# Top-16 search moved in among the query products, one-hots in four operations, and another order of loads

## The reference

```python
mod = cond @ w_ada[l] + b_ada[l]                 # 6 * 1024 values, sh1, sc1, g1, sh2, sc2, g2
q = (hf @ w_q).reshape(T, PEER_HEADS, 2, D_HALF) # 8 heads, 2 halves of 128
s = jnp.einsum("thpd,hpkd->thpk", q, sub_keys)   # 128 scores per half
top_v, top_i = lax.top_k(s, PEER_TOPK)           # the first top-16, 16 per token
comb = top_v[:, :, 0, :, None] + top_v[:, :, 1, None, :]   # 256 sums a head
best_v, best_j = lax.top_k(comb.reshape(T, PEER_HEADS, 256), PEER_TOPK)   # the second
i1 = jnp.take_along_axis(top_i[:, :, 0], best_j // PEER_TOPK, axis=-1)
i2 = jnp.take_along_axis(top_i[:, :, 1], best_j % PEER_TOPK, axis=-1)
idx, gate = i1 * N_KEYS + i2, jax.nn.softmax(best_v)       # 128 experts a token
a = jnp.einsum("tmd,td->tm", u_tab[idx], x)
y = jnp.einsum("tm,tmd->td", gate * jax.nn.gelu(a, approximate=False), v_tab[idx])
```

## Time and profile before

| what | us |
|---|---|
| runs shown, median (lowest, highest) | 3184.18 (3183.21, 3186.78) |
| profiled execution | 3189.15 |
| its span, granted clock 0.987 | 3187.3 |
| PE busy | 3091.1 |
| DVE busy | 2457.8 |
| POOL busy | 1185.7 |
| ACT busy | 1118.5 |

### The profile page before, as it was taken

One profiled execution on the slowest core, in us unless ns is written; L12 is line 12 of the kernel. 1 busy time (PEld: TensorE's weight loads), 2 busy tenths in 40 slices (PEclk: granted clock), 3 DMA queues, 4 the chain that ended last, 5 costly groups with the idle time before them and its releaser, 6 DMA issues.

```text
span 3187.3 us, 54768 instructions
## 1 busy us (share of the span) xinstructions
PE 3091.1 (97%) x16200; PEld 2682.7 (84%) x16200; DVE 2457.8 (77%) x5952; ACT 1118.5 (35%) x1590; POOL 1185.7 (37%) x765
## 2 busy tenths in 40 slices
PE   6989999999999999999999999999999999999998
PEld 4668888778888899999975788888788889999997
DVE  7981999859995488999977239951799926889987
ACT  3333322234443333333343332223344433333333
POOL 0033445420001366766700334544000024667674
PEclk8999999999999999999999999999999999999999
DMA  6162666445556799999921224444455578999996
GB/s 254 62 216 101 241 231 240 165 139 188 215 207 256 254 362 361 360 361 363 374 91 40 85 82 142 147 145 141 149 218 210 189 287 293 362 358 361 361 371 238
DMA packets 278481, 734.76 MB, mean 231 GB/s; under 512 B 36064, under 2 KB 118368, under 8 KB 276448
## 3 DMA queue, kind: packets, MB, share of 16 engines
q1 hardware_dynamic: 186688, 462.03, 41.7%
q0 software_dynamic: 50688, 151.18, 12.8%
q10 hardware_dynamic: 40992, 120.34, 9.6%
HBM read 613.85 MB, written 119.54 MB: 230 GB/s over the span
## 4 chain that ended last, share of the span: by engine, by line
PE 54%; POOL 18%; issue 14%; DVE 10%; DMA 2%; ACTq 1%; ACT 1%; DVEq 0%; SPq 0%; POOLq 0%
PE bank L507 30%; PE bank L511 15%; POOL z_pad L934 9%; POOL u_pad L928 5%; PE bank L616 3%; POOL z_pad L928 2%; POOL scratch L928 2%; PE bank L528 2%; DVE scratch L1285 2%; PE bank L427 1%; ACTq L826 1%; DVE h L1266 1%; DVE h L1263 1%; PE bank L451 1%; DVE h L1265 1%
## 5 line engine op out<-in xcount | busy, mean ns | idle before, releaser
L507 PE MATMUL bank<-h_hi,w_hi 128*128 128x512 f32 x2528 | 997.9, 395 | 19.2 <-ACT norm_tmp L807 16.3
L673 ACT ACTIVATE w_hi<-ring 128x1024 fp32r<-128x1024 f32 x584 | 615.0, 1053 | 1116.0 <-PE bank L511 1036.8
L507 PE MATMUL bank<-h_lo,w_hi 128*128 128x512 f32 x2528 | 988.2, 391 | 0.0
L913 POOL TENSOR_TENSOR w_lo<-ring,w_hi 128x1024 fp32r<-128x1024 f32 x172 | 442.8, 2575 | 844.2 <-ACT w_hi L673 844.1
L633 PE MATMUL bank<-v_lo,w_hi 128*128 128x368 f32 x2032 | 670.5, 330 | 0.0
L633 PE MATMUL bank<-v_hi,w_hi 128*128 128x368 f32 x2032 | 665.2, 327 | 2.7 <-DVE v_lo L1439 1.8
L511 PE MATMUL bank<-h_hi,w_lo 128*128 128x512 f32 x2528 | 624.3, 389 | 0.0
L507 PEld LDWEIGHTS bank<-h_hi,w_hi 128*128 128x128 f32 x2528 | 476.9, 189 | 119.4 <-ACT w_hi L673 19.1
L507 PEld LDWEIGHTS bank<-h_lo,w_hi 128*128 128x128 f32 x2528 | 476.7, 189 | 97.1
L511 PEld LDWEIGHTS bank<-h_hi,w_lo 128*128 128x128 f32 x2528 | 474.5, 188 | 98.6
L934 POOL DMA_INDIRECT z_pad<-ga_scratch,z_pad x288 | 374.0, 1299 | 155.0 <-issue 86.9
(11 more groups left out here) (184 smaller groups left out, 2885.0 us busy)
## 6 DMA issues: line engine op xcount, KB each, us to landing
ring<-u_t SPq DMA_DIRECT2D x256, 512.0 KB
ring<-v_t SPq DMA_DIRECT2D x256, 512.0 KB
ga_scratch<-norm_tmp ACTq DMA_DIRECT2D x256, 256.0 KB, 2.0
g_scratch<-scratch ACTq DMA_DIRECT2D x12, 4096.0 KB, 13.8
scratch<-ga_scratch SPq DMA_DIRECT2D x256, 192.0 KB
scratch<-ada_t SPq DMA_DIRECT2D x76, 512.0 KB, 5.8
scratch<-g_scratch SPq DMA_DIRECT2D x32, 768.0 KB
keys<-g_scratch SPq DMA_DIRECT2D x32, 768.0 KB
```

The source lines that it names most:

```text
L507: pe.matmul(to, w_hi[:, b, k * P:(k + 1) * P], part_h[:, k, :], start=(k == 0 and part_h is h_hi), stop=False)
L673: return act.activation(to, of, ACT.Copy)
L913: pool.tensor_tensor(w_lo[:, n % 2, :], ring[:, n % RING, :], w_hi[:, n % 2, :].bitcast(F32), ALU.subtract).then_inc(tile_used[n % RING], 1)
```

## The change

Five things change.

1. PE multiplies a segment with its keys right behind the query product two tiles later (`score(n - 2)`), all four token tiles at once, into banks 0 and 1. ACT copies it one step later (`copy_score`). DVE takes the first top-16 of two segments, 8 rows, as soon as both are there.
2. The second top-16 looks at 100 sums a head instead of 256: the first 3 ranks with all 16, the other 13 with the first 4.
3. The look-up of both halves is one comparison and one product over 4096 fp16 elements, then additions of halves.
4. The one-hots of a chunk come from four instructions of 1024 elements. `hot1` now has two tokens side by side, so that PE reads every second fp16.
5. The last eight slices of layer 0 leave the query stage. They take the first turn of the eight slots, and layer 1's 48 follow, four for each four up chunks, starting at the second four. DVE uses them in groups of 5, 5 and 4.

```diff
     NEXT_SLOTS = 8
-    NEXT_FROM = 3
-    NEXT_ROUNDS = (N_ADA - NEXT_SLOTS) // RING
+    NEXT_FROM, PER_ROUND = 1, 4
+    OWN_ADA = KC
+    N_NEXT = OWN_ADA + N_ADA
+    NEXT_ROUNDS = (N_NEXT - NEXT_SLOTS) // PER_ROUND
...
+                def load_own(s):
+
+                    sp.wait_ge(next_used[s], N_NEXT // NEXT_SLOTS * l + 1)
+                    sp.dma_start(ada_next[:, s, :], ada_t[l, N_ADA - OWN_ADA + s]).then_inc(next_landed[s], 16)
...
                 up_rounds(0, 1)
                 with sp.If(l < LAST):
-                    sp.wait_ge(score_ready, 4 * TT * l + 4 * TT)
+                    sp.wait_ge(score_ready, SEGS * l + SEGS)
                     for s in range(NEXT_SLOTS):
-                        load_next(0 * l, s)
+                        load_own(s)
                     settle(sp)
-                    up_rounds(1, NEXT_FROM)
-                    with sp.Fori(0, NEXT_ROUNDS // 2) as q:
-                        for half in range(2):
-                            for s in range(RING):
-                                load_next(q + 1, RING * half + s)
-                            up_round(2 * q + (NEXT_FROM + half))
+                    with sp.Fori(0, NEXT_ROUNDS // 4) as q:
+                        for half in range(4):
+                            for i in range(PER_ROUND * half, PER_ROUND * (half + 1)):
+                                load_next(2 * q + (i // NEXT_SLOTS + 1), i % NEXT_SLOTS)
+                            up_round(4 * q + (NEXT_FROM + half))
...
+                def score(s):
+
+                    pe.wait_ge(q_ready, N_WQ * l + (s + 1))
+                    if s >= 2:
+                        pe.wait_ge(score_ready, SEGS * l + (s - 1))
+                    for a in range(TT):
+                        mm = pe.matmul(bank[:, s % 2, a * P:(a + 1) * P], q_t[:, s, a * P:(a + 1) * P], keys_v[:, s, :],
+                                       start=True, stop=True)
+                    mm.then_inc(score_product, 1)
...
                     product(l, 0, stages["wq"] + n, bank[:, 2 + n % 6, :])
...
+                    score(n - 2)
+                score(N_WQ - 2)
+                score(N_WQ - 1)
...
                 for n in range(N_WQ):
                     hi(0, stages["wq"] + n + 2)
                     copy(q_t[:, n, :], bank[:, 2 + n % 6, :]).then_inc(q_ready, 1)
...
+                    if n >= 3:
+                        copy_score(n - 3)
+                for s in range(N_WQ - 3, N_WQ):
+                    copy_score(s)
...
-                with dve.If(l < 1):
-                    for n in range(KC):
-                        modulate_later(3 * KC + n)
-                wait_later(LATER)
-                add_bias(5 * KC, KC)
...
+                for pair in range(SEGS // 2):
...
+                    dve.wait_ge(score_ready, SEGS * l + (2 * pair + 2))
+                    settle(dve)
+                    top16(PAIR, lambda n: scores[:, seg(n)[1], seg(n)[0], :], lambda n: big_s[:, n, :],
+                          lambda n: vals[:, seg(n)[0], seg(n)[1], :], lambda n: idx_u[:, seg(n)[0], seg(n)[1], :])
...
                     top16(HEADS, lambda s: big_c[:, s, :], lambda s: sc_c[:, s, :], lambda s: best[:, s, :],
                           lambda s: bj_v[:, s, :])
-                    next_modulation(3 if a < TT - 1 else 2)
...
+                    next_modulation(5)
...
+                    link(dve.tensor_tensor(eq_4, ranks.unsqueeze(2).to_broadcast(shape4),
+                                           iota_rank.unsqueeze(1).to_broadcast(shape4), ALU.is_equal))
+                    link(dve.tensor_tensor(eq_4, eq_4, idx_h.unsqueeze(3).to_broadcast(shape4), ALU.mult))
+                    next_modulation(5)
+                    half = TOPK // 2
+                    while half > 1:
+                        link(dve.tensor_tensor(eq_4[:, :, 0:half, :], eq_4[:, :, 0:half, :], eq_4[:, :, half:2 * half, :],
+                                               ALU.add))
+                        half //= 2
...
-                        for j in range(TOK):
-                            t = RING * TOK * r + (s * TOK + j)
-                            col = bass.ds(t, 1)
-                            dve.tensor_scalar(hot2[:, b, j, :], iota_b[:, :], i2_t[:, col], None, ALU.is_equal)
-                            for q, g_part in enumerate((ghi_t, glo_t)):
-                                ins = dve.tensor_scalar(hot1[:, b, j, q, :], iota_b[:, :], i1_t[:, col], g_part[:, col],
-                                                        ALU.is_equal, ALU.mult)
-                        ins.then_inc(hot_ready, 1)
...
+                        dve.tensor_tensor(hot1[:, b, 1, :, :, :], table, along(i1_t), ALU.is_equal).then_inc(hot_step, 1)
+                        dve.tensor_tensor(hot2[:, b, :, :], iota_b[:, :].unsqueeze(1).to_broadcast([P, TOK, P]),
+                                          i2_t[:, cols].unsqueeze(2).to_broadcast([P, TOK, P]), ALU.is_equal)
+                        dve.wait_ge(hot_step, LATE * l + RING * r + s + 1)
+                        dve.tensor_tensor(hot1[:, b, 0, :, :, :], hot1[:, b, 1, :, :, :], along(ghi_t), ALU.mult)
+                        dve.tensor_tensor(hot1[:, b, 1, :, :, :], hot1[:, b, 1, :, :, :], along(glo_t), ALU.mult)\
+                           .then_inc(hot_ready, 1)
```

More of the change, by code:

```diff
@@ L614, in _ @@
                             to = bank[:, 2 + 2 * b + j // PER_BANK, (j % PER_BANK) * P:(j % PER_BANK + 1) * P]
+                            g, i = j // SIDE, j % SIDE
                             for q in range(2):
-                                mm = pe.matmul(to, hot2[:, b, j, :], hot1[:, b, j, q, :], start=(q == 0), stop=(q == 1))
+                                mm = pe.matmul(to, hot2[:, b, j, :], hot1[:, b, q, g, :, i], start=(q == 0), stop=(q == 1))
                         mm.then_inc(gate_product, 1)
@@ L791, in _, with copy_score @@
                 shift_hi(2 * l + 1, 3 * KC)
+                def copy_score(s):
+                    act.wait_ge(score_product, SEGS * l + (s + 1))
+                    copy(scores[:, :, s, :], bank[:, s % 2, :].rearrange("p (a k) -> p a k", k=P)).then_inc(score_ready, 1)
                 for n in range(N_WQ):
@@ L794, in _ @@
                     copy(q_t[:, n, :], bank[:, 2 + n % 6, :]).then_inc(q_ready, 1)
-                for s in range(LATER_SLOTS):
-                    act.wait_ge(later_used[s], LATER // LATER_SLOTS + 1)
-                for a in range(TT):
-                    for b in range(4):
-                        act.wait_ge(score_product, 4 * TT * l + (4 * a + b + 1))
-                        copy(scores[:, a, 4 * b:4 * b + 4, :],
-                             bank[:, 4 * (a % 2) + b, :].rearrange("p (s k) -> p s k", k=P)).then_inc(score_ready, 1)
+                    if n >= 3:
+                        copy_score(n - 3)
+                for s in range(N_WQ - 3, N_WQ):
+                    copy_score(s)
                 def gelu(r, s):
@@ L1287, in next_modulation @@
                                .then_inc(next_used[slot], 1)
                     nexts[0] += n
-                for a in range(TT):
-                    dve.wait_ge(score_ready, 4 * TT * l + 4 * (a + 1))
-                    settle(dve)
-                    sc_a = scores[:, a, :, :]
-                    sc_c = sc_a.rearrange("p s k -> p (s k)").rearrange("p (s k) -> p s k", k=TOPK * TOPK)
-                    top16(SEGS, lambda s: sc_a[:, s, :], lambda s: big_s[:, s, :], lambda s: vals[:, s, :],
-                          lambda s: idx_u[:, s, :])
-                    next_modulation(4 if a < TT - 1 else 3)
-                    link(dve.tensor_tensor(big_4, v2[:, :, 0, :].unsqueeze(3).to_broadcast(shape4),
-                                           v2[:, :, 1, :].unsqueeze(2).to_broadcast(shape4), ALU.add))
+                    if nexts[0] - n < OWN_ADA <= nexts[0]:
+                        settle(dve)
+                        with dve.If(l < LAST):
+                            for slot in range(OWN_ADA):
+                                dve.wait_ge(next_used[slot], N_NEXT // NEXT_SLOTS * l + 2)
+                            settle(dve)
+                        add_bias(5 * KC, KC)
@@ new lines, in _ @@
+                    count(dve.tensor_copy(idx_h[:, :, :], idx_u[:, :, a, :]))
+                    count(dve.tensor_copy(j_f, bj))
+                    dve.wait_ge(dve_step, STEPS * l + (FIRST + steps[0] - 2))
+                    count(dve.tensor_copy(ja_f, ja_u))
+                    link(dve.tensor_copy(jb_f, jb_u))
+                    link(dve.scalar_tensor_tensor(ja_f, jb_f, float(ROWS_WIDE - at // NARROW), ja_f, ALU.add, ALU.max))
+                    count(dve.tensor_copy(ranks_2[:, :, 0, :], heads(ja_f)))
@@ L1318, in _ @@
+                    for e, to in enumerate((i1_f, i2_f)):
+                        ins = dve.tensor_tensor(heads(to[:, a, :]), eq_2[:, :, e, 0, :], eq_2[:, :, e, 1, :], ALU.add)
+                        count(ins)
```

(3 more changed lines are left out.)

138 lines of the change are left out of this document (73 added, 65 removed).

## The result

| | before | after |
|---|---|---|
| median of runs, us (lowest, highest, number) | 3185.48 (3183.21, 3188.43, 4) | 3210.80 (3209.55, 3215.13, 4) |
| profiled execution | 3189.15 | 3211.41 |
| its span, granted clock | 3187.3, 0.987 | 3209.6, 0.984 |
| layer 0's up stage, first up product to first one-hot matmul | 360.08 | 381.43 |
| the same in layer 1 | 355.10 | 355.10 |

What follows compares the result with a forecast made beforehand. PE was taken to bound the kernel, other engines mattering only where PE waits. Terms 22.3 + 2.2 - 5.0 + 0.9 gave +20.4 us, put on the median 3184.18: 3204 us, range 3193 to 3215.

Steps and rivals of the forecast that it cites:

- One-hots: In the 96 one-hot chunks PE sets the pace at 6.45 us, DVE needs at most 6.1: 0 us.
- Rival 3: SP's gate stops PE, but the one-hot chunks give back their 9 us: 3195 us, chance 0.04.
- Moving operand with a step of two: PE reading hot1 at every second fp16 in the small matmuls costs nothing: 0 us.
- The other end, +88: PE reading the spaced one-hot operand at half pace in all 96 chunks would cost 88 us.
- Scores amid the products: At the query stage's end, saved idle time returns as waits on ACT's copies: +0.4 us a layer.
- Both top-16s: In the up stage DVE's lighter top-16 work stays hidden, as ACT still asks at chunk 56: no gain.
- SP's queue: Layer 0's fifth u_t tile waits behind gated slice requests, so PE stops 22.3 us; with clock and old stop, +19.5 us.
- The lower bound of 18 for the stop: Shortest forecast PE stop before layer 0's fifth up chunk: 18 us, with 9.3 us a pair and no queueing.
- Lower clock: After the stop in layer 0's up stage PE runs at its lower level for a while: +2.2 us.
- The stop before 588: PE's old 3.1 us wait in layer 0's up stage goes, with 1.9 more: 5.0 us given back.
- Rival 1: SP's gate does not bite, DVE having used slot 3 by 336.7: 3180 us, chance 0.07, plus 0.03 for faster.
- Rival 2: New one-hots cost PE or DVE: +88 us (3292) for half-pace reads or +370 for slow operations; chance 0.05 together.

Runs made afterwards that it cites:

- kernel 4: The kernel before the change with only the four-operation one-hots put in; 3185.83 us, ratio 1.0006 to the kernel before.
- kernel 1: The changed kernel with the gated slices one round later on SP's queue (NEXT_FROM = 2); 3190.66 us, ratio 1.0017 to the kernel before.
- kernel 3: The changed kernel with DVE using five slices ahead of the sums and second top-16 instead of behind; 3206.77 us, ratio 1.0065 to the kernel before.
- kernel 2: The changed kernel with the gated slices two rounds later on SP's queue (NEXT_FROM = 3); 3183.65 us, ratio 0.9996 to the kernel before.

## Why the prediction held, step by step

The mechanism, its place and its side came out as forecast: 3210.8 us against 3204, in the range. The trace grew by 22.3 us (3209.6 against 3187.3) where the sum had 20.4. It is that close in part by luck: the stop, the lower clock and the one-hots came out 3.1 us above their terms, the queries 1.7 below theirs.

- **One-hots, 0 us.** Right. A chunk went from 6.447 to 6.460, 1.2 us over all 96, which kernel 4 shows apart from the rest. The bound of 6.1 us for DVE was a loose one: from the start of the low half to the end of the last operation it is 4.2. Rival 3, that 9 us come back, is out: DVE has 2.3 us to spare and the chunk did not get shorter.
- **Moving operand with a step of two, 0 us.** Right. The 16 small matmuls take 1.10 us instead of 1.07, which is 0.002 us each. The other end, +88, would have been 0.057 each. The Trainium skill, page SBUF — State Buffer, section Door 1, says that a stride is free while at least two reads fall in each 16-byte line; the trace agrees, to within these 0.03 us a chunk.
- **Scores amid the products, +0.4 us a layer.** The one term with the wrong sign. The stage is 0.4 us shorter (106.01 against 106.42 us, in layer 1 107.10 against 107.49). Half of that is the stage's first product, 0.2 us shorter in each layer, which varies from profile to profile (5.2 us in kernel 4, 5.5 in kernel 1) and is none of the scores' doing; behind it stand 100.8 us against 101.0. The 0.05 us that I allowed for each change of operand kind is not there: a segment costs 0.91 alone or between products. The end was worked out well: 5.56 us against 5.45.
- **Both top-16s, hidden.** Right. DVE's wait for the exponential went from 90.6 to 225.0 us, and no part of that shows in PE's time.
- **SP's queue, +19.5 us.** Right in mechanism; the stop was 23.9 us, not 22.3. Three sizes in it were off.
  - A pair takes 10.45 us (323.61 to 334.05), not 9.8: the gaps of some 0.1 us between its five groups of operations, and the settling step of 0.2 (an instruction without work between two groups), are now paid for every 8 rows and not for every 16, which is a part of it. The first top-16s ended at 344.4 all the same, against the 344.3 worked out, and that was luck: the sixth pair began at 313.1 and not 314.9, and 1.0 of these 1.8 us is only that the whole query stage began earlier (216.66 against 217.66).
  - The second top-16, from 345.58 to 355.32 with its settling step, takes 9.7 us and not 8.7. I had drawn a line through 8 rows of 256 (15.9) and of 128 (9.8). The point at 128 was 0.45 too low (10.25 without the settling step), and DVE pauses for 0.47 us ahead of the second eight maxima, at 351.57, where a pair pauses for 0.1.
  - PE wanted the tile at 344.6, not 346.3. Of this, 1.0 is again the earlier start, which moves DVE too and leaves the stop as it is.

  The product came 7.5 us behind the tile's request (360.98 to 368.45) against 8.6, so the 1 us added for crowding was too much. Counted from the start of the query stage, the request came 2.0 us later than worked out, PE's need 0.7 earlier, the product 1.1 sooner behind the request: 22.3 becomes 23.9. Tile 8 was asked for at 379.13, some 6 us before it would have stopped PE; this is the margin that kernel 3 used up. The lower bound of 18 for the stop does not follow from its conditions: 0.5 off each of three pairs and 1 off the landing give 19.8. The range did not rest on it.
- **Lower clock, +2.2.** 2.5 by the table.
- **The stop before 588, −5.0.** Right in the traces: layer 0's up stage is 5.0 us longer before than in kernel 2, and the stop is absent in kernels 1 to 3 as in the kernel after; with the one-hots alone it stays. These kernels have the shorter retrieval, the earlier first top-16s and the split into groups of five together. Which of the three removes it was not taken apart, and the medians of kernel 2 don't show the whole gain.
- **The rivals.** Rival 1, the gate does not bite, needed DVE to have used slot 3 by 336.7; it did at 360.0. Rival 2 is out by kernel 4, whose interval ends 0.15% (5 us) above the kernel before.

What the steps leave open is a few microseconds. The changed places add up to +21.4 for the up stage, −0.8 for the queries and +1.2 for the one-hots: 21.8 of the 22.3 in the spans. Between the medians it is 25.3, with an interval of 20.4 to 31.5 from the ratio. The profiled execution before lay 4 us above the median of its runs and the one after 0.6, so that part goes with the scatter between executions; no mechanism for it is shown.

## What to carry to other kernels

On a queue that issues in order, a request that waits for a slot is a gate for everything behind it, so place it by when the engine that frees the slot will get there at the earliest, worked out with its backlog, and not by how many requests are to be spread. Where the work of an engine is cut by a tenth and the engine above it sets the pace, the saving turns up as idle time. After such a stop look along the queue for the next gate: a shorter stop only moves the moment at which the next tile is wanted.

## What was not expected of the hardware

- **DVE at half the time for fp16, and when not.** From start to start an operation of 1024 fp16 elements takes 0.61 us (773.03 to 773.64, 774.77 to 775.38), but L1421, of the same size and type, 1.13 (773.64 to 774.77). It is the one whose second operand stands still along the innermost axis; in the others the two tokens lie side by side and each step reads another element. The Trainium skill, page VectorE: DVE Perf Modes, section What auto-detection actually checks, says that the mode of two elements at a time needs every tensor at 16 bits with a step of one. The trace agrees: 0.61 with it, 1.13 without.
- **DVE beside POOL.** A slice of the modulation takes 1.22 us while POOL rests (the gated ones above) and 3.4 us while POOL is making a low half. Two neighbours show the border: the one that began 0.7 us ahead of POOL took 1.21, the next one, begun inside POOL's operation, 3.41.

```profile
376.95 1.21 DVE L1306 SCALAR_TENSOR_TENSOR scratch<-scratch,cond 128x1024 f32<-128x1024 f32 x1
...
378.10 3.41 DVE L1306 SCALAR_TENSOR_TENSOR scratch<-scratch,cond 128x1024 f32<-128x1024 f32 x1
```

```profile
377.69 2.73 POOL L926 TENSOR_TENSOR w_lo<-ring,w_hi 128x1024 fp32r<-128x1024 f32 x1 [1.76 <-ACT w_hi L684]
```

  During the stop POOL has nothing to do, and all four gated slices run at 1.22 or 1.23. In kernel 1, where PE and POOL keep running, the third of them took 3.41. So the stop shortens itself a little.
- **Issuing is work.** ACT takes 0.64 us for each small DMA that it issues (15.35 over 24). Four at a time in chunks in which ACT has 3.9 us idle, they cost PE nothing: its chunks there take what they take in kernel 2 (5.44 us, and 6.78 for the one in which PE turns indices and gates over).
